# Rotary turn of queries and keys: the exchange of half heads moved from a TensorE permutation to transfers issued by ScalarE

## The reference, cut to what matters

```
def rope(x, cos, sin):            # x: (B, S, heads, 64)
    x1, x2 = jnp.split(xf, 2, axis=-1)
    return concatenate([x1 * cos - x2 * sin, x2 * cos + x1 * sin])
...
k_shared = rope(kv[:, :, 0], cos, sin)            # 4 key heads
q = rope((h @ w_q[j]).reshape(B, S, 16, 64), cos, sin)   # 16 query heads
```

## Time and profile before

| | |
|---|---|
| median of three runs | 2337.47 us |
| profiled execution, own time | 2336.23 us |
| its span in the profile | 2334.5 us |
| busy PE, DVE, ACT, POOL (page, part 1) | 99%, 63%, 45%, 15% |
| stage of keys, queries and the first units | about 453 to 532 us of the span |

### The profile page before, as it was taken

One profiled execution on the slowest core, in us unless ns is written; L12 is line 12 of the kernel. 1 busy time (PEld: TensorE's weight loads), 2 busy tenths in 40 slices (PEclk: granted clock), 3 DMA queues, 4 the chain that ended last, 5 costly groups with the idle time before them and its releaser, 6 DMA issues. The chain is left out here.

```text
span 2334.5 us, 35165 instructions
## 1 busy us (share of the span) xinstructions
PE 2300.8 (99%) x13026; PEld 1947.4 (83%) x13026; DVE 1470.7 (63%) x2157; ACT 1059.9 (45%) x1728; POOL 349.4 (15%) x380
## 2 busy tenths in 40 slices
PE   9999999999999999999999999999999999999998
PEld 8888888967988888898788888888878789888887
DVE  5785788698688768869545334337578745432433
ACT  6643554556465334644354223326456533421421
POOL 0120121111322212210010000010136621000001
PEclk9999999999999999999999999999999999999999
DMA  5455553232345555444123223222312122222221
GB/s 215 142 180 195 176 184 126 77 118 73 136 162 181 177 173 187 175 183 170 55 91 103 95 90 108 90 81 94 110 56 75 39 91 91 90 103 95 90 96 66
DMA packets 56348, 282.52 MB, mean 121 GB/s; under 512 B 7996, under 2 KB 19008, under 8 KB 28336
## 3 DMA queue, kind: packets, MB, share of 16 engines
q1 hardware_dynamic: 34144, 213.85, 25.9%
q0 software_dynamic: 12560, 58.80, 7.4%
q10 hardware_dynamic: 9536, 8.39, 1.1%
HBM read 265.15 MB, written 15.86 MB: 120 GB/s over the span
## 5 line engine op out<-in xcount | busy, mean ns | idle before, releaser
L2200 DVE TENSOR_TENSOR w_lo<-raw,w_hi 128x1024 fp32r<-128x1024 f32 x386 | 504.0, 1343 | 400.7 <-ACT w_hi L1339 400.5
L1339 ACT ACTIVATE w_hi<-raw 128x1024 fp32r<-128x1024 f32 x386 | 388.8, 1053 | 417.1 <-PE ps L526 402.3
L524 PE MATMUL ps<-h_hi,w_hi 128*128 128x512 f32 (+1 forms) x1312 | 464.4, 354 | 3.8 <-DVE h_lo L2273 1.5
L525 PE MATMUL ps<-h_lo,w_hi 128*128 128x512 f32 (+1 forms) x1312 | 454.5, 346 | 0.0
L526 PE MATMUL ps<-h_hi,w_lo 128*128 128x512 f32 (+1 forms) x1312 | 454.4, 346 | 0.0
L524 PEld LDWEIGHTS ps<-h_hi,w_hi 128*128 128x128 f32 x1312 | 248.4, 189 | 44.2 <-issue 8.0
L530 PE MATMUL ps<-h_hi,w_hi 128*128 128x512 f32 (+1 forms) x720 | 274.1, 383 | 0.7 <-DVE h_lo L2964 0.7
L525 PEld LDWEIGHTS ps<-h_lo,w_hi 128*128 128x128 f32 x1312 | 248.4, 189 | 31.2 <-issue 0.7
L526 PEld LDWEIGHTS ps<-h_hi,w_lo 128*128 128x128 f32 x1312 | 248.2, 189 | 30.7
L531 PE MATMUL ps<-h_lo,w_hi 128*128 128x512 f32 (+1 forms) x720 | 273.4, 382 | 0.0
L3281 POOL TENSOR_TENSOR sqsum<-sqsum,sq 128x256 f32<-128x256 f32 (+1 forms) x84 | 91.9, 1094 | 968.1 <-issue 595.9
(11 more groups left out here) (436 smaller groups left out, 3501.5 us busy)
## 6 DMA issues: line engine op xcount, KB each, us to landing
raw<-weights_dram SPq DMA_DIRECT2D x161, 1024.0 KB, 4.8
ada_w<-ada_dram POOLq DMA_DIRECT2D x48, 1024.0 KB, 5.1
raw<-weights_dram SPq DMA_DIRECT2D x32, 704.0 KB, 4.0
par<-par_dram SPq DMA_DIRECT2D x8, 1152.0 KB, 7.1
par_dram<-plane POOLq DMA_DIRECT2D x10, 512.0 KB, 3.8
tab<-tab_dram SPq DMA_DIRECT2D x8, 512.0 KB, 7.4
x_tok<-x_rows_dram SPq DMA_DIRECT2D x4, 512.0 KB, 5.2
x<-x_in_dram SPq DMA_DIRECT2D x1, 2048.0 KB, 14.3
```

The costliest lines, as they stand in the source:

```text
L524: nc.tensor.matmul(dst, w_hi[:, o:o + P], rhs_hi, start=start, stop=False)
L525: nc.tensor.matmul(dst, w_hi[:, o:o + P], rhs_lo, start=False, stop=False)
L1339: nc.scalar.activation(w_hi[:, o:o + TILE // 2], raw[:, o:o + TILE // 2], ACT.Copy).then_inc(w_hi_done, 1)
L2200: nc.vector.tensor_tensor(w_lo[:, o], raw[:, o], w_hi[:, o].bitcast(f32), SUB).then_inc(w_split, 1)
```

## The change: exchange by transfers, product in place, sum on GpSimd

The permutation on PE goes, with its constant and its load, and so do the products' waits for it. ACT issues, behind the copy of each part to SBUF, four transfers of 32 partitions x 512 numbers (64 KB each) from the raw part to `gl`, every one to the partitions of the other half of its head. It first waits until the part two before has been added up, because that part's `gl` is overwritten, and then for its own copy. DVE makes the cosine product as before, waits for the four transfers, and multiplies `gl` by the sine in place. The sum is made by POOL (`rope_add`), in a queue with the stores of the S5 planes: four adds, the two stores of plane 0, and then an add and a store in turn. PE's query parts from part 2 on wait for ACT's copy of the part two before instead of DVE's sine product.

```
@@ PE
-            pe.wait_ge(sem("qraw"), C["qraw"].after())
-            nc.tensor.matmul(bank(b), perm[:, :], src, start=True, stop=True).then_inc(sem("rot"), 1)
...
-                pe.wait_ge(sem("rope_parts"), 2 * t + m + 1)
+                pe.wait_ge(sem("qraw"), 2 * t + m + 1)
...
-        query_part(0, 1, {2: keys_turned})
-        rope_part(6, chunk(tg, 0))
-        rope_part(7, chunk(tg, 1))
+        query_part(0, 1)
...
-            rope_part(6 + s % 2, chunk(tg, s % 2))
@@ ACT
+        def halves_swapped(n, m, src):
+
+            if n > 2:
+                act.wait_ge(rope_done, n - 2)
+            act.wait_ge(qraw, n)
+            for i in range(4):
+                here, there = slice(32 * i, 32 * i + 32), slice(32 * (i ^ 1), 32 * (i ^ 1) + 32)
+                act.dma_start(chunk(gl, m)[here], src[there]).then_inc(sem(f"swapped{m}"), 16)
...
+        for m in range(2):
+            halves_swapped(m + 1, m, key_raw(m))
...
+            halves_swapped(2 * t + m + 3, m, chunk(tg, m))
@@ DVE
-        def rope(b, m, src, dst):
-
-            dve.wait_ge(sem("qraw"), C["qraw"].after())
+        def rope(n, m, src):
+
+            dve.wait_ge(sem("qraw"), n)
+            if n > 2:
+                dve.wait_ge(sem("rope_done"), n - 2)
             nc.vector.tensor_tensor(chunk(tv, m), src, cosT[:, :], MUL)
-            dve.wait_ge(sem("rot"), C["qraw"].now())
-            nc.vector.tensor_tensor(chunk(gl, m), bank(b), sinT[:, :], MUL).then_inc(sem("rope_parts"), 1)
-            dve.wait_ge(sem("rope_parts"), C["qraw"].now())
-            nc.vector.tensor_tensor(dst, chunk(tv, m), chunk(gl, m), ADD).then_inc(sem("rope_done"), 1)
+            dve.wait_ge(sem(f"swapped{m}"), 64 * ((n + 1) // 2))
+            nc.vector.tensor_tensor(chunk(gl, m), chunk(gl, m), sinT[:, :], MUL).then_inc(sem("rope_parts"), 1)
@@ POOL
-        for n in range(4):
-            for part in range(2):
-                store5(n, part)
+        def rope_add(n, dst):
+
+            m = (n - 1) % 2
+            gp.wait_ge(sem("rope_parts"), n)
+            gp.tensor_tensor(dst, chunk(tv, m), chunk(gl, m), ADD).then_inc(sem("rope_done"), 1)
+
+        for m in range(2):
+            rope_add(m + 1, chunk(sq, m))
+        for p in range(2):
+            rope_add(p + 3, chunk(q, p))
+        store5(0, 0)
+        store5(0, 1)
+        for p in range(2, DC):
+            rope_add(p + 3, chunk(q, p))
+            store5(p // 2, p % 2)
@@ SP
-                sp.dma_start(perm[:, :], consts[:, P:2 * P]).then_inc(sem("tables_landed"), 16)
```

More of the change, by code:

```diff
@@ L197, in build @@
     mod_at = place("mod_at", 2)
-    ident, perm, ones = place("ident", P), place("perm", P), place("ones", P)
+    ident, ones = place("ident", P), place("ones", P)
     at[0] = (at[0] + 31) // 32 * 32
@@ L782, in ffn @@
                 second_norm()
-        def rope_part(b, src):
-            pe.wait_ge(sem("qraw"), C["qraw"].after())
-            nc.tensor.matmul(bank(b), perm[:, :], src, start=True, stop=True).then_inc(sem("rot"), 1)
         pe.wait_ge(sem("pool_set"), POOL_SET["ones"])
@@ L844, in _ @@
         kept_busy(6)
-        pe.wait_ge(sem("tables_landed"), 48)
+        pe.wait_ge(sem("tables_landed"), 32)
         starts("kproj")
@@ L963, in weighed @@
             if j == EARLY:
-                pe.wait_ge(sem("rope_parts"), 10)
+                pe.wait_ge(sem("qraw"), 10)
                 kept_busy(9, output_bank(j), 0)
@@ L1740, in _ @@
         g.after()
-        act.wait_ge(sem("tables_landed"), 48)
+        act.wait_ge(sem("tables_landed"), 32)
         act.wait_ge(sem("pool_set"), POOL_SET["planes"])
@@ L2564, in rope_angles @@
         def rope_angles():
-            dve.wait_ge(sem("tables_landed"), 48)
+            dve.wait_ge(sem("tables_landed"), 32)
             chain(nc.vector.tensor_copy(cosT[:, :], posi[:, :]))
@@ L2784, in _ @@
         dve.wait_ge(sem("angles"), 2)
-        def rope(b, m, src, dst):
-            dve.wait_ge(sem("qraw"), C["qraw"].after())
+        def rope(n, m, src):
+            dve.wait_ge(sem("qraw"), n)
+            if n > 2:
+                dve.wait_ge(sem("rope_done"), n - 2)
             nc.vector.tensor_tensor(chunk(tv, m), src, cosT[:, :], MUL)
-            dve.wait_ge(sem("rot"), C["qraw"].now())
-            nc.vector.tensor_tensor(chunk(gl, m), bank(b), sinT[:, :], MUL).then_inc(sem("rope_parts"), 1)
-            dve.wait_ge(sem("rope_parts"), C["qraw"].now())
-            nc.vector.tensor_tensor(dst, chunk(tv, m), chunk(gl, m), ADD).then_inc(sem("rope_done"), 1)
+            dve.wait_ge(sem(f"swapped{m}"), 64 * ((n + 1) // 2))
+            nc.vector.tensor_tensor(chunk(gl, m), chunk(gl, m), sinT[:, :], MUL).then_inc(sem("rope_parts"), 1)
         def query_rope(p):
-            rope(6 + p % 2, p % 2, chunk(tg, p % 2), chunk(q, p))
-        rope(4, 0, key_raw(0), chunk(sq, 0))
-        rope(5, 1, key_raw(1), chunk(sq, 1))
+            rope(p + 3, p % 2, chunk(tg, p % 2))
+        rope(1, 0, key_raw(0))
+        rope(2, 1, key_raw(1))
         g.after()
```

## The result

The changed kernel takes 2344.1 us (median of six runs, 2343.36 to 2348.34); the kernel before, on the same chip, takes 2336.86 (2335.64 to 2337.6). The ratio is 1.0036, with a 95% interval of 1.0026 to 1.0046: slower by 6 to 11 us, where 2336.5 was forecast. The profiled execution took 2343.36 us, its span is 2341.7.

What follows compares the result with a forecast made beforehand. PE is busiest overall, but DVE is nearly as busy in this stage and limits the sum. Gaining 1.0 us at the last transposition gives span 2333.5, profiled execution 2335.2, and, 1.24 above it, median 2336.5; range 2331.5 to 2343.

Steps and rivals of the forecast that it cites:

- the issue on ACT: ACT's transfer issues: 0.33 us each, 1.32 for four, 2.64 for the keys' eight; upper bound 0.78 each.
- the walk of the prediction: Schedule through the stage: first scores 472.6, first transposition 484.2, scores behind the last rotation 525.1, next transposition 526.3.
- GpSimd's hold: DVE's instruction behind each rotation stands 1.10 us during GpSimd's add; add saved 0.72, so a step takes 8.83, not 8.45.
- the first rival: GpSimd's add doesn't hold DVE (0 for 1.10): step 7.7, time 2331.0; unslowed weight splits would prove it; chance 0.12.
- Landing: Exchange transfers land 2.2 us after the last issue, bounds 2.2 to 7.1.
- The second rival: Exchanges land late, up to 7.1 us: 2345; each microsecond beyond 2.2 counts about twice, less 1.4 slack; chance 0.14.
- the third rival: PE's new waits lower its clock; a query part at 1.2 GHz takes 5.5 longer, less waits: 2339.5; chance 0.16.
- The end: The transposition behind the last rotation's scores starts at 526.3, before held till 527.29: 1.0 us gained.
- What PE gained: The ten permutation products taken off PE are worth 9 to 9.5 us if PE alone were the limit.

Runs made afterwards that it cites:

- e4: The changed kernel with one transfer of 128 partitions an exchange instead of four, same bytes, halves not exchanged so the output differs: 2338.06 us, ratio 1.0008.
- e9: The changed kernel with eight transfers of 32 KB an exchange instead of four of 64 KB, same bytes: 2365.73 us, ratio 1.0129.
- e3: The kernel before, permutation still on PE, with only the sum moved from DVE to GpSimd: 2339.02 us, ratio 1.0011.
- e11: The changed kernel with one transfer an exchange (halves not exchanged, output differs) and the sum back on DVE: 2335.3 us, ratio 0.9997.

## Why the prediction was wrong, step by step

**The step that failed is the issue on ACT.** The prediction took 0.33 us each "since ACT's queue is empty here", so 1.32 for an exchange and 2.64 for the keys'. Measured: 0.61 each, 2.44, and 6.95 for the keys' eight (0.87 each). The upper bound of the earlier trace rows, 0.78, was nearer; the row chosen was that of a store of which there are two, and the empty queue was an assumption. By the keys' issues ACT was 4.3 us late, by those of parts 0 and 1 another 1.1 each, and about one of these 6.5 us fell into a wait; the last issue of part 1 ended at 472.5 instead of 467.05, the key copies began 5.2 late, and the first scores came at 478.43 instead of 472.6. These 5.8 us were carried unchanged through four steps (rotation of part 2 at 484.28, not 478.45; of part 5 at 510.74, not 504.9). The copies of the keys wait in ACT's queue behind the issues, and this delay had been priced at 2.64 of ACT's time with slack behind it. e4 shows it: with 0.47 us an exchange the walk of the prediction comes out within about a microsecond up to the last transposes, and the time is 1.8 above the kernel before instead of 1.0 below; e9 shows the other direction.

The walk also lacked two waits at the start. DVE waits 1.68 us for the keys' exchange, and PE, which was to begin part 2 at once at 464.8, waits 1.82 for the weight split that DVE makes behind it and begins at 467.15. How much of this is issue and how much landing isn't separated: e4, with its keys' landing of 7.1, still has 1.11 of the first. PE ends part 2 at 472.9 instead of 470.5, still ahead of what the first scores wait for.

The Trainium skill (DMA: Bandwidth & Descriptors, Issuing engines are not separate DMA queues) says that the time a sequencer takes to initiate a transfer is usually small beside the transfer. This case's trace bears it out for one transfer only loosely, with 0.61 us of issue against 2.1 to landing, and not for several in a row: the four issues of an exchange take 2.44 us one behind the other, longer than the 2.1 in which a transfer lands.

**GpSimd's hold: right in size, one instruction late.** 1.10 forecast; the product beside the add takes 1.78 instead of 0.69, and the step is 8.80 where 8.83 was forecast. The prediction looked for it in the weight split and took an unslowed split as proof of the first rival (no hold). In the loop the split is unslowed, 1.22, since the add starts just behind its start (485.66 and 485.49), and the next instruction pays; the length of the step and e3 refute that rival, and its sign was badly chosen. That the add contends with DVE at all is what the Trainium skill says (SBUF — State Buffer, Who interferes with whom); the trace agrees on the contention and shows half of the add's 2.19 us as its price.

**Landing: right for the parts, low for the start.** Median 2.1 forecast 2.2; 3.6 for the keys, whose exchange runs beside weight loads, and 3.3 for part 1 (last issue ends at 472.5, DVE goes on at 475.86). That accounts for 0.6 of the first scores' delay: they follow GpSimd's add of part 1, which ends at 478.28, not the key copies, which end at 477.68. The second rival, a late exchange, had the right place and the wrong reason: it blamed the landing at up to 7.1, and it was the issue. Its rule of about two microseconds for each one of landing, less 1.4, doesn't fit: part 1's exchange came 6.6 us after the forecast's landing, which gives 11.8, and the last transposes were 8.2 behind the forecast.

**The clock: the third rival holds in part.** Behind the wait of 5.50 us the granted clock was 0.50, the 1.2 GHz level, for about five microseconds of PE's work, the scores and the start of part 3. The changed kernel's stretches of two microseconds:

```profile
474.00:476.00 2.00, 0.00 (x0) 0.00 (x0) 0.14 (x1) 1.95 (x4) 0.00 (x0) 1.00 0.41 118
476.00:478.00 2.00, 0.00 (x0) 0.00 (x0) 2.00 (x3) 1.95 (x4) 1.36 (x1) 0.68 0.00 0
478.00:480.00 2.00, 1.57 (x10) 1.38 (x10) 1.95 (x3) 1.25 (x2) 0.28 (x1) 0.50 0.00 0
480.00:482.00 2.00, 2.00 (x8) 1.49 (x7) 1.94 (x4) 0.14 (x1) 0.96 (x1) 0.50 0.37 88
482.00:484.00 2.00, 2.00 (x7) 1.53 (x7) 1.89 (x5) 1.14 (x1) 0.70 (x1) 0.61 0.97 275
484.00:486.00 2.00, 2.00 (x10) 1.65 (x9) 1.97 (x5) 1.61 (x10) 0.53 (x2) 1.00 0.71 212
```

It fell in the last two microseconds of the wait and came back some five microseconds after PE had work again. This low stretch cost little in the profiled run, since DVE set the pace of that step; the wait at the first transposes was 0.98 instead of the 3.4 forecast for a clock that stays up. But it adds what the prediction didn't have: scatter. Over 28 runs the kernel before went from 2334.3 to 2337.2 at clocks of 0.995 to 0.997; e4, beside it, from 2335.17 at 0.997 to 2341.09 at 0.992.

**The end.** Forecast -1.0 at the last transposition, measured +7.2. Of the 8.2 between them 5.8 come from the start, and most of the rest from the exchange of part 6: its four issues took 3.26 instead of 1.32, it landed at 522.09, and DVE waited 1.74.

**What PE gained: right, and worth nothing.** PE is busy 5.7 us less, the products being worth 9 to 9.5 and the low clock taking some back, and e11 shows that even with cheap issues this gives no more than -0.0003 (0.0006 to -0.0012): behind an engine that is busy 9.7 of 10 us, freed time of PE mostly makes its waits longer, as the prediction said. Behind the two long waits of e11 the clock is at 0.50, which the prediction had only in its third rival.

## What to carry to other kernels

Price a DMA issue as an instruction of the engine that issues it, by a row of the same kind (several in a row, SBUF to SBUF), multiply by their number, and follow what stands behind them in that queue; if only rows far apart are there, put the higher one on the path first. An exchange that an idle-looking engine issues in four pieces was worth some 6.5 us of delay, while its landing was hidden in most of the later steps. And before moving work off the busiest engine, ask which engine ends the waits now: here freed PE time turned into waits, and those were followed by a lower clock. Products that are to fill a wait are priced by their row too: forty were taken for 5.0 us, lasted 8.85, and held up the work that they stood in front of.

## What of the hardware was not expected

- An issue on ACT took 0.61 us when several follow each other, with 32 KB as with 64 KB; 0.47 for one alone of 256 KB and 128 partitions; 0.87 on average when eight followed each other beside weight loads. On two queues at once two took 1.41.
- Landings of 256 KB between two places of SBUF were 2.5 us in the query parts and 7.1 for the keys in e4, as long as the slow row; DVE waited only 1.1 for it.
- GpSimd's add of 128 x 512 takes 1.6 to 2.2 us beside a busy DVE and 1.25 where DVE reads PSUM and then idles (at 531.68 in the changed kernel).
- A wait of PE of 5.5 us was followed by about five microseconds of work at the 1.2 GHz level. With small products in it the clock stayed up there, and lower clocks appeared in two later stretches.
- A small product of 128 x 128 in a row of forty took 0.22 us at a granted clock of 1.00.
